# Key columns taken into the first modulation, a wide first MLP product, and a last panel that finishes token tile 0 first

## The chip, the cores and the metric

One core of one Trainium2 chip. The metric is the device time of one execution in microseconds (us); lower is better. Everything is float32 data; products run on TensorE (PE) in fp32r, each operand split into a high part (rounded to fp32r) and a low part (the rest), so that one product of the reference becomes three matmuls: high by high, high by low, low by high.

## What is computed

One layer of a trunk over 256 context and 256 latent tokens, width 2048 (biases, gates' details and norms left out):

```
mod_l, mod_c = silu(c) @ w_ada + b_ada, silu(c_ctx) @ w_ada + b_ada     # 6 x 2048 each
ul, uc  = (xl * (1 + sc1_l) + sh1_l) @ w_in, (xc * (1 + sc1_c) + sh1_c) @ w_in
ya, yb, yc = hgrn(uc, ul), pool(ul), attention(uc, ul)                  # attention: q, k, v are columns of w_in
xl = LayerNorm(ALPHA * xl + g1_l * (sum_j sigmoid(gate_j) * (y_j @ w_branch_j)) @ w_out)
h  = xl * (1 + sc2_l) + sh2_l
xl = LayerNorm(ALPHA * xl + g2_l * (square(relu(h @ w_ff1)) @ w_ff2))   # w_ff1 2048 x 8192
```

## The kernel before

All weights (395 MB) stream once from HBM in chunks of 1 MB: 512 rows by 512 columns, laid out 128 partitions x 4 row tiles x 512 columns. SyncE issues their DMAs in one fixed order (`stream()`), into a ring of eight slots during the first modulation and of four after it; each DMA waits until the chunk that held its slot is used up. Four chunks along the rows make a panel of 512 output columns.

A chunk of kind "s" is split in two halves: ScalarE (ACT) copies a half to `whi` (L405), VectorE (DVE) subtracts it from the raw half into `wlo` (L847), TensorE multiplies. `whi` and `wlo` hold four halves; a half's place is free when TensorE has ended the half four before it (counted by `w_used`, or by `blk_done` for a panel's last half). Chunks of kind "p" (`ada`) are the first two sixths of w_ada and are multiplied raw by a 32-column vector operand (L1356); ACT copies the sums out (`sums_out`, L426), TensorE turns them (`turn`, L1365), DVE makes the modulated inputs, whose high and low parts are `hCL`, context and latent side by side (512 columns). Chunks of kind "a" are the rest of w_ada and are summed on DVE (`ada_sum`, L865 and L868), beside later panels.

The first stage has four rounds `kc`, each with eight `ada` chunks. From the second on, a round also multiplies one chunk of the first value panel (`value_block`, L1375 to L1377), from inputs that the round before has modulated. ACT's order in a round is: sums out, split of the value chunk, sums out, high parts of `hCL`. After it come value chunk 3, the second value panel, then the panel of attention keys and values (L1285 to L1287 for the keys, L1453 to L1457 for the values), then 4 "forget" panels, queries, gates, branches, the output projection, and the MLP.

The MLP has four rounds `f`. In each, four panels of w_ff1 go through `features` (L1285 to L1287): the weights are the stationary operand, 128 columns at a time, the 256 latent tokens are the moving one. DVE takes each result through relu (L1189) into `sq`, GpSimd (POOL) squares it and makes its two parts `hid` (L831, L724, L726). Then four panels of w_ff2 go through `tokens` (L1324 to L1326): `hid` is stationary, 512 weight columns move, two token tiles `t` of 128 rows each. A tokens panel takes chunk n only when the `hid` rows of feature panel n are done, so the first of them needs the last feature panel's `hid` at its chunk 3. In the last panel of all, chunks 2 and 3 are done for tile 0 first and then for tile 1 (`apart=2`), so that DVE's closing work on tile 0 (`ff_out`, L1200 to L1207; `last_rows`, L1214 and L1216) runs beside tile 1.

Of the kernel before, what the change touches and what calls it, by code (L numbers as in the profile page):

```python
# [52 lines left out]
class Stream:  # L53
# [4 lines left out]
    def __init__(self):  # L58
        self.order, self.place, self.nth = [], {}, {}
        self.count = {"s": 0, "p": 0, "a": 0}  # L60
        self.split_order = []
# [3 lines left out]
    def add(self, kind, name, n, src, index):  # L65
# [9 lines left out]
        if kind == "s":  # L75
            self.split_order.append((name, n))

# [6 lines left out]
    def half(self, name, n, h):  # L84
        return 2 * self.nth[name, n] + h
# [6 lines left out]
def stream():  # L92
# [27 lines left out]
    for n, pan in enumerate((PAN_AI + 1, PAN_CKV)):  # L120
        for k in range(4):
            panel("vals", 4 + 4 * n, k, "w_in", 4 * pan + k)
            summed()
            summed()
    for n in range(16):
        panel("forget", n, 0, "w_in", 4 * PAN_AF + n)
        summed()
    for n in range(8):
# [28 lines left out]
class Panels:  # L157
# [8 lines left out]

    def add(self, name, first, chunks, banks, who):
# [15 lines left out]

def panels():
    pn = Panels()
    four = (0, 1, 2, 3)
    for first in (0, 4, 8):
        pn.add("vals", first, 4, four, "A")
# [13 lines left out]
    for f in range(4):  # L202
        for i in range(4):
            pn.add("mlp", 32 * f + 4 * i, 4, four, "V")
# [8 lines left out]
def build(nc, vecs, cst, rcnt, masks, xT, xtok, rows, w_ada, w_in, pool_w, w_br, w_out, w_f1, w_f2, outT):  # L213
    weights_of = {"w_ada": w_ada, "w_in": w_in, "w_br": w_br, "w_out": w_out, "w_f1": w_f1, "w_f2": w_f2}
    with ExitStack() as ctx:
# [11 lines left out]
        wlo = at("wlo", [P, 4, 2, PW], 48 * KB, F32R)  # L227

# [89 lines left out]
        def sem(name):  # L318
# [12 lines left out]
         m_tr, m_hi, m_lo, ax_in, var_in, rs_out, nm_out, h2_tr, h2_hi, h2_lo, x1_done, hid_lo, y_out, cleared) = (  # L331
# [5 lines left out]
            "m_tr m_hi m_lo ax_in var_in rs_out nm_out h2_tr h2_hi h2_lo x1_done hid_lo y_out cleared").split())  # L337
# [32 lines left out]
        def _(sp):  # L370
            for n, (kind, name, k, src, index) in enumerate(ST.order):
# [4 lines left out]
                if ST.holder[n] is not None:  # L376
# [3 lines left out]
                    elif was == "s":  # L380
                        sp.wait_ge(lo_made, ST.half(old, o, 1) + 1)
# [3 lines left out]
                sp.dma_start(slots[slot][:].rearrange("p a b -> p (a b)"),  # L385
# [7 lines left out]
        def _(act):  # L393
# [3 lines left out]
            def split(name, n, halves=(0, 1)):  # L397
                slot = ST.slot(name, n)
                act.wait_ge(raw_full[slot], ST.full(name, n))
                for h in halves:  # L400
# [4 lines left out]
                    nc.scalar.copy(whi[:, q % 4], slots[slot][:, 2 * h:2 * h + 2]).then_inc(hi_made, 1)  # L405
# [1336 lines left out]
```

## Time and profile before

| | |
|---|---|
| median of 3 runs | 1952.09 us (1946.99 to 1952.15) |
| the profiled execution | 1952.81 us, of which the traced span is 1951.0 us |
| TensorE busy | 1885.7 us (97%) |
| VectorE busy | 1258.3 us (64%) |
| ScalarE busy | 777.3 us (40%) |
| GpSimd busy | 389.3 us (20%) |
| HBM traffic | 409.04 MB, mean 210 GB/s |

TensorE's time runs through the whole span. In the timeline a matmul's length is its way through the array, longer than the distance between two starts; that distance is what one costs in a row of them, and is read from the starts.

### The profile page before, as it was taken

What the parts mean: (1) busy time and instruction counts of PE and PEld (TensorE: products, weight loads), DVE (VectorE), ACT (ScalarE), POOL (GpSimd) and SP (SyncE); (2) the same over time, 40 slices, a digit from 0 to 9 for tenths busy, and PEclk for the clock granted to TensorE, in tenths of its full rate; (3) what the DMA queues carried; (4) which work ended last, traced back from release to release, by engine and by line L of the source; (5) the groups of instructions that cost most, each with busy time, mean ns of one, the idle gap of its engine ahead of it and who ended that gap; (6) DMA issues with size and microseconds to landing.
All of it is one profiled execution on the core that took longest, in us unless ns stands there. A gap on an engine that the chain in (4) does not pass through costs nothing.

```text
span 1951.0 us, 26303 instructions
## 1 busy us (share of the span) xinstructions
PE 1885.7 (97%) x10808; PEld 1624.0 (83%) x10808; DVE 1258.3 (64%) x1438; ACT 777.3 (40%) x891; POOL 389.3 (20%) x325
## 2 busy tenths in 40 slices
PE   5999999999999999999999998999999999999996
PEld 1568887889999877887888887998998899889985
DVE  1247646786877776487676666766676467556686
ACT  1132224455555554444444435433333333333331
POOL 0000000002837343100010100450054024203500
PEclk7889999999999999999999999999999999999998
DMA  9957745555343454476676754666665566556652
GB/s 400 421 200 271 261 170 173 173 177 188 111 142 106 136 212 159 143 275 221 232 273 235 273 199 168 219 221 203 244 236 197 196 214 235 194 194 224 230 175 84
DMA packets 59319, 409.04 MB, mean 210 GB/s; under 512 B 6336, under 2 KB 9024, under 8 KB 10304
## 3 DMA queue, kind: packets, MB, share of 16 engines
q1 hardware_dynamic: 54720, 395.34, 57.2%
q10 hardware_dynamic: 4480, 12.02, 1.6%
q8 instruction: 86, 1.41, 0.3%
q14 instruction: 33, 0.27, 0.0%
HBM read 405.24 MB, written 2.10 MB: 209 GB/s over the span
## 4 chain that ended last, share of the span: by engine, by line
PE 86%; DVE 7%; DMA 2%; POOL 1%; DVEq 1%; issue 1%; ACT 1%; SPq 0%; ACTq 0%
PE main L1324 14%; PE main L1326 14%; PE main L1325 14%; PE main L1285 11%; PE main L1286 11%; PE main L1287 11%; DVE asum L868 2%; DMA raw<-in_w_ada 2%; PE main L1375 2%; DVE wlo L847 2%; PE main L1376 2%; PE main L1377 2%; PE side L1356 1%; PE side L1519 1%; PE side L1589 1%
## 5 line engine op out<-in xcount | busy, mean ns | idle before, releaser
L847 DVE TENSOR_TENSOR wlo<-raw,whi 128x1024 fp32r<-128x1024 f32 x552 | 722.3, 1334 | 329.8 <-ACT whi L405 329.2
L405 ACT CAST whi<-raw 128x1024 fp32r<-128x1024 f32 x552 | 574.1, 1050 | 792.8 <-PE main L1326 421.3
L1285 PE MATMUL main<-h,whi 128*128 128x256 f32 x1024 | 291.5, 285 | 4.6 <-DVE h L1180 2.5
L1286 PE MATMUL main<-h,whi 128*128 128x256 f32 x1024 | 291.1, 284 | 0.0
L1287 PE MATMUL main<-h,wlo 128*128 128x256 f32 x1024 | 291.0, 284 | 0.0
L1285 PE MATMUL main<-hCL,whi 128*128 128x256 f32 (+1 forms) x800 | 261.9, 327 | 7.1 <-DVE ya L1030 3.6
L1286 PE MATMUL main<-hCL,whi 128*128 128x256 f32 (+1 forms) x800 | 258.4, 323 | 0.0
L1287 PE MATMUL main<-hCL,wlo 128*128 128x256 f32 (+1 forms) x800 | 258.2, 323 | 0.0
L868 DVE SCALAR_TENSOR_TENSOR asum<-raw,sm,asum 128x512 f32<-128x512 f32 x240 | 192.6, 802 | 19.5 <-issue 0.4
L1324 PE MATMUL main<-whi,hid 128*128 128x512 f32 x512 | 201.2, 393 | 0.9 <-DVE wlo L847 0.9
L1285 PEld LDWEIGHTS main<-h,whi 128*128 128x128 f32 x1024 | 197.8, 193 | 5.1 <-DVE h L1180 2.8
L1325 PE MATMUL main<-wlo,hid 128*128 128x512 f32 x512 | 199.5, 390 | 0.0
L1326 PE MATMUL main<-whi,hid 128*128 128x512 f32 x512 | 199.5, 390 | 0.0
L1286 PEld LDWEIGHTS main<-h,whi 128*128 128x128 f32 x1024 | 197.7, 193 | 0.1
L1287 PEld LDWEIGHTS main<-h,wlo 128*128 128x128 f32 x1024 | 197.8, 193 | 0.0
L831 POOL TENSOR_TENSOR sq<-sq 128x256 f32<-128x256 f32 x64 | 67.5, 1055 | 535.6 <-DVE sq L1189 528.0
L1285 PEld LDWEIGHTS main<-hCL,whi 128*128 128x128 f32 x800 | 153.4, 192 | 18.9 <-issue 6.5
L1286 PEld LDWEIGHTS main<-hCL,whi 128*128 128x128 f32 x800 | 153.5, 192 | 11.2 <-issue 0.2
L1287 PEld LDWEIGHTS main<-hCL,wlo 128*128 128x128 f32 x800 | 153.3, 192 | 11.4
L1324 PE MATMUL main<-whi,hCL 128*128 128x512 f32 x384 | 156.2, 407 | 0.4 <-DVE wlo L847 0.4
L1326 PE MATMUL main<-whi,hCL 128*128 128x512 f32 x384 | 150.0, 391 | 0.0
L1325 PE MATMUL main<-wlo,hCL 128*128 128x512 f32 x384 | 149.8, 390 | 0.0
(226 smaller groups left out, 2631.2 us busy)
## 6 DMA issues: line engine op xcount, KB each, us to landing
raw<-in_w_f SPq DMA_DIRECT2D x128, 1024.0 KB, 4.9
raw<-in_w_in SPq DMA_DIRECT2D x108, 1024.0 KB, 4.9
raw<-in_w_ada SPq DMA_DIRECT2D x96, 1024.0 KB, 6.2
raw<-in_w_br SPq DMA_DIRECT2D x24, 1024.0 KB, 5.0
raw<-in_w_out SPq DMA_DIRECT2D x16, 1024.0 KB, 5.0
xin<-in_xT SPq DMA_DIRECT2D x4, 1024.0 KB, 18.2
ax<-in_xtok ACTq DMA_DIRECT2D x1, 2048.0 KB, 8.4
lng<-in_rows ACTq DMA_DIRECT2D x2, 1024.0 KB, 7.1
```

The lines of the kernel that those rows point to most:

```text
L405: nc.scalar.copy(whi[:, q % 4], slots[slot][:, 2 * h:2 * h + 2]).then_inc(hi_made, 1)
L831: TT(sq[:, b], sq[:, b], sq[:, b], ALU.mult)
L847: TT(wlo[:, q % 4], slots[slot][:, 2 * h:2 * h + 2], whi[:, q % 4].bitcast(F32), ALU.subtract).then_inc(lo_made, 1)
L868: last = STT(asum[:], slots[slot][:, j], s, asum[:], ALU.mult, ALU.add)
L1285: mm(out, w_hi, x_hi, start=start, stop=False)
L1286: mm(out, w_hi, x_lo, start=False, stop=False)
L1287: return mm(out, w_lo, x_hi, start=False, stop=stop)
L1324: mm(out, x[:, kt, 0, own], whi[:, par, j], start=start, stop=False)
L1325: mm(out, x[:, kt, 0, own], wlo[:, par, j], start=False, stop=False)
L1326: last = mm(out, x[:, kt, 1, own], whi[:, par, j], start=False, stop=stop)
L1375: mm(main[:, b], x[:, kt, 0, tile], whi[:, par, j], start=kt == 0, stop=False)
L1376: mm(main[:, b], x[:, kt, 0, tile], wlo[:, par, j], start=False, stop=False)
```

## The change

Three parts. **Keys:** the 512-column panel of attention keys and values is cut in two kinds of chunks: four `keys` chunks of half a megabyte (512 rows by 256 columns, one half each) and two `cv` chunks of 1 MB (1024 rows by 256 columns). Key chunks 0 to 2 are streamed, split and multiplied in the first stage, chunk 3 after value chunk 3; in PSUM they have banks 2 and 3 of `side`, and the modulation sums keep only bank 1, where they had 1 and 2. **Wide:** `features` in the MLP is replaced by `wide`; its results have the high-part and low-part sums in two halves of a bank, which ACT and DVE add, and the panels alternate between `main` and `side`. Squares are made by ACT (high part) and GpSimd. **Tail:** `apart=4` in the last panel, with places of their own for its last four halves (`whi_end`, `wlo_end`, where `h2` was).

```diff
@@ stream() @@
         if kc:
             panel("vals", 0, kc - 1, "w_in", 4 * PAN_AI + kc - 1)
+            st.add("s", "keys", kc - 1, "w_ck", kc - 1, halves=1)
...
+    st.add("s", "keys", 3, "w_ck", 3, halves=1)
@@ panels() @@
-            pn.add("mlp", 32 * f + 4 * i, 4, four, "V")
+            pn.add("mlp", 32 * f + 4 * i, 4, (four, SIDE)[i % 2], "V")
@@ scalar: split @@
-                    if q >= 4:
+                    if q == HALVES - 4:
+                        act.wait_ge(blk_done, PN.base["mlp", 108] + 4)
+                    elif 4 <= q < HALVES - 4:
                         which, count = PN.last[q - 4]
                         act.wait_ge(ended[which], count)
@@ scalar: first stage @@
-                nc.scalar.copy(am[:, n % 2], side[:, 1 + n % 2]).then_inc(am_out, 1)
+                nc.scalar.copy(am[:, n % 2], side[:, 1]).then_inc(am_out, 1)
...
                 split("vals", kc - 1)
+                split("keys", kc - 1)
@@ scalar: MLP @@
+            def hidden_in(f, i):
+                if f or i:
+                    act.wait_ge(hid_lo, 4 * f + i)
+                for b in range(4):
+                    blk("mlp", 32 * f + 4 * i, b)
+                    nc.scalar.copy(sq[:, b], (main, side)[i % 2][:, b, 0:T]).then_inc(hid_in, 1)
+
+            def hidden_high(f, i):
+                act.wait_ge(hid_pos, 4 * f + i + 1)
+                A(hid[:, 4 * i:4 * i + 4, 0], sq[:], ACT.Square).then_inc(hid_hi, 1)
...
                         split_after("mlp", 32 * f + n)
+                    if n in (4, 8, 12, 16):
+                        hidden_in(f, n // 4 - 1)
+                    if n in (5, 9, 13, 17):
+                        hidden_high(f, n // 4 - 1)
@@ gpsimd: MLP @@
+            for n in range(16):
+                pool.wait_ge(hid_hi, n + 1)
+                TT(sq[:], sq[:], sq[:], ALU.mult)
+                drain()
+                own = slice(n % 4 * 4, n % 4 * 4 + 4)
+                TT(hid[:, own, 1], sq[:], hid[:, own, 0].bitcast(F32), ALU.subtract).then_inc(hid_lo, 1)
@@ vector: hidden_out @@
-                    nc.vector.tensor_scalar_max(sq[:, b], main[:, b, 0:T], 0.0).then_inc(freed["V"], 1)
+                    dve.wait_ge(hid_in, 16 * f + 4 * i + b + 1)
+                    TT(sq[:, b], sq[:, b], (main, side)[i % 2][:, b, T:2 * T], ALU.add).then_inc(freed["V"], 1)
+                drain()
+                nc.vector.tensor_scalar_max(sq[:], sq[:], 0.0).then_inc(hid_pos, 1)
@@ tensor: new wide() @@
+                            for j in range(2):
+                                kt, own = 4 * n + 2 * h + j, slice(P * b, P * (b + 1))
+                                mm(ps[:, b], whi[:, par, j, own], h2[:, kt].rearrange("p v t -> p (v t)"),
+                                   start=kt == 0, stop=kt == 15, skip_group_check=True)
+                                last = mm(ps[:, b, 0:T], wlo[:, par, j, own], h2[:, kt, 0], start=False,
+                                          stop=kt == 15, skip_group_check=True)
@@ tensor: first stage @@
             for kc in range(1, 4):
                 for k in range(4):
                     ada_chunk(8 * kc + k)
+                    if kc > 1:
+                        key_block(kc - 2, k)
...
+            for k in range(4):
+                key_block(2, k)
@@ tensor: MLP @@
-                           between=lambda k: ada_spread(12 + f) if i == 0 and k == 0 else None,
-                           apart=2 if f == i == 3 else 0)
+                           between=lambda k: gate2(f) if i == 0 and k == 1 else None,
+                           apart=4 if f == i == 3 else 0)
```

Left out of the diff: the bookkeeping of halves, the new host layouts `w_ck` and `w_cv`, four of the `ada_sum` chunks that move from the panel of keys and values to the first forget panel (with two of their turns), DVE's matching splits, and the waits on the freed banks.

On TensorE, at the start of the third round of the first stage (`raw` is a slot, `side` bank 1 takes the modulation sums): four `ada` chunks before, then the value chunk.

```order
L1356 MATMUL side<-raw_50,sR 32x512 x4
L1356 MATMUL side<-raw_51,sR 32x512 x4
L1356 MATMUL side<-raw_52,sR 32x512 x4
L1356 MATMUL side<-raw_53,sR 32x512 x4
L1375 MATMUL main<-whi,hCL 128x512
```

The same place in the change, its first `ada` chunk and what follows.

```order
L1455 MATMUL side<-raw_51,sR 32x512 x4
L1360 MATMUL side<-hCL,whi 128x512
L1361 MATMUL side<-hCL,whi 128x512
L1362 MATMUL side<-hCL,wlo 128x512
L1360 MATMUL side<-hCL,whi 128x512
L1361 MATMUL side<-hCL,whi 128x512
L1362 MATMUL side<-hCL,wlo 128x512
L1455 MATMUL side<-raw_52,sR 32x512 x4
```

A quarter of a key chunk, six matmuls of 512 columns, stands behind each of the four `ada` chunks, the last of them ahead of the value chunk.

On TensorE, in the first feature panel of the MLP, before:

```order
L1285 MATMUL main<-h_79,whi 128x256
L1286 MATMUL main<-h_79,whi 128x256
L1287 MATMUL main<-h_79,wlo 128x256
L1285 MATMUL main<-h_79,whi 128x256
L1286 MATMUL main<-h_79,whi 128x256
L1287 MATMUL main<-h_79,wlo 128x256
```

And in the change:

```order
L1400 MATMUL main<-h_81,whi 128x512
L1402 MATMUL main<-h_81,wlo 128x256
L1400 MATMUL main<-h_81,whi 128x512
L1402 MATMUL main<-h_81,wlo 128x256
L1400 MATMUL main<-h_81,whi 128x512
```

Two matmuls stand where three stood, with the same 768 columns in all.

On GpSimd, the work for one feature panel before is four times these three rows:

```order
L831 TENSOR_TENSOR sq<-sq 128x256
L724 TENSOR_TENSOR hid<-sq,ones 128x256
L726 TENSOR_TENSOR hid<-sq,hid 128x256
L831 TENSOR_TENSOR sq<-sq 128x256
L724 TENSOR_TENSOR hid<-sq,ones 128x256
L726 TENSOR_TENSOR hid<-sq,hid 128x256
```

In the change it is these first two rows (and they repeat for each panel):

```order
L904 TENSOR_TENSOR sq<-sq 128x1024
L907 TENSOR_TENSOR hid<-sq,hid 128x4x256
L904 TENSOR_TENSOR sq<-sq 128x1024
L907 TENSOR_TENSOR hid<-sq,hid 128x4x256
L904 TENSOR_TENSOR sq<-sq 128x1024
```

Two operations of 1024 elements stand where twelve of 256 stood, and they start only when ACT's square of all four blocks is done.

## Rows read from the trace of the kernel before

**Rows 1.** The page: span, and TensorE's busy time (share, instructions)

```profile
span 1951.0 us, 26303 instructions
PE 1885.7 (97%) x10808; PEld 1624.0 (83%) x10808; DVE 1258.3 (64%) x1438; ACT 777.3 (40%) x891; POOL 389.3 (20%) x325
```

**Rows 2.** TensorE's waits, whole span: us in total, times, longest

```profile
PE main L1375 <- DVE wlo L847: 9.0, 3, 3.0
```

**Rows 3.** Stretches of the first stage: length, busy times, then PEclk, DMA share, GB/s

```profile
66.30:95.50 29.20, 26.20 (x130) 14.12 (x129) 8.06 (x17) 5.54 (x8) 0.00 (x0) 0.82 1.01 421
...
74.00:84.30 10.30, 10.30 (x36) 5.09 (x35) 0.00 (x0) 0.00 (x0) 0.00 (x0) 0.50 1.02 422
...
103.00:112.40 9.40, 9.40 (x35) 4.98 (x34) 2.40 (x3) 0.58 (x1) 0.00 (x0) 0.54 0.17 72
```

**Rows 4.** TensorE's timeline, first stage: start, length, what [idle before]

```profile
55.78 0.40 PE L1377 MATMUL main<-whi,hCL 128*128 128x512 f32 x1
56.11 1.07 PE L1356 MATMUL side<-raw,sR 128*32 128x512 f32 x8
57.11 0.50 PE L1375 MATMUL main<-whi,hCL 128*128 128x512 f32 x1
57.44 0.39 PE L1376 MATMUL main<-wlo,hCL 128*128 128x512 f32 x1
...
66.32 3.64 PE L1356 MATMUL side<-raw,sR 128*32 128x512 f32 x32
72.96 0.47 PE L1375 MATMUL main<-whi,hCL 128*128 128x512 f32 x1 [3.00 <-DVE wlo L847]
...
125.53 0.50 PE L1375 MATMUL main<-whi,hCL 128*128 128x512 f32 x1 [1.19 <-DVE hCL L902]
```

**Rows 5.** TensorE's timeline, MLP: 16 starts of 256 columns, 96 of 512

```profile
1212.03 0.28 PE L1287 MATMUL main<-h,wlo 128*128 128x256 f32 x1
...
1213.83 0.28 PE L1287 MATMUL main<-h,wlo 128*128 128x256 f32 x1
...
1912.37 0.39 PE L1324 MATMUL main<-whi,hid 128*128 128x512 f32 x1
...
1933.90 0.39 PE L1326 MATMUL main<-whi,hid 128*128 128x512 f32 x1
```

**Rows 6.** Two other idle times, and the granted clock around them

```profile
1229.40 0.36 PE L1285 MATMUL main<-h,whi 128*128 128x256 f32 x1 [2.05 <-DVE wlo L847]
...
1221.40:1235.00 13.60, 11.55 (x97) 11.38 (x96) 10.71 (x15) 7.76 (x11) 1.09 (x2) 1.00 0.66 233
...
319.50 1.70 PE L1469 MATMUL side<-cs,kctx 128*128 128x128 f32 x8 [2.57 <-ACT kctx L479]
...
320.00:330.00 10.00, 10.00 (x41) 0.84 0.32 105
```

**Rows 7.** Groups of DVE; then the squares' chain around 1304.34 (tokens start)

```profile
L1189 DVE TENSOR_SCALAR sq<-main 128x256 f32<-128x256 f32 x64 | 27.2, 425 | 35.3 <-PE main L1287 35.3
...
L868 DVE SCALAR_TENSOR_TENSOR asum<-raw,sm,asum 128x512 f32<-128x512 f32 x240 | 192.6, 802 | 19.5 <-issue 0.4
...
1310.01 1.05 ACT L405 CAST whi<-raw 128x1024 fp32r<-128x1024 f32 x1 [1.61 <-PE main L1326]
...
1302.96 0.61 POOL L831 TENSOR_TENSOR sq<-sq 128x256 f32<-128x256 f32 x1 [9.61 <-DVE sq L1189]
...
1305.37 1.40 POOL L831 TENSOR_TENSOR sq<-sq 128x256 f32<-128x256 f32 x1 [0.16 <-issue]
...
L779 POOL TENSOR_TENSOR qr<-qr,qs x2: 2377/2790/3204, 670.1 to 781.7; 128x1024 f32<-128x1024 f32 x2
```

**Rows 8.** DVE's timeline over the last panel and behind it

```profile
1915.51 4.81 DVE L847 TENSOR_TENSOR wlo<-raw,whi 128x1024 fp32r<-128x1024 f32 x4
...
1928.96 0.69 DVE L1200 TENSOR_TENSOR res<-main,g2b 128x512 f32<-128x512 f32 x1 [3.20 <-PE main L1326]
...
1938.68 0.68 DVE L1200 TENSOR_TENSOR res<-main,g2b 128x512 f32<-128x512 f32 x1
```

More of the change, by code:

```diff
@@ L76, in add @@
             self.split_order.append((name, n))
+            first = sum(count for _, count in self.halves.values())
+            self.halves[name, n] = (first, halves)
     def slot(self, name, n):
@@ L84, in half, with halves_of, split @@
     def half(self, name, n, h):
-        return 2 * self.nth[name, n] + h
+        return self.halves[name, n][0] + h
+    def halves_of(self, name, n):
+        return range(self.halves[name, n][1])
+    def split(self, name, n):
+        return sum(self.halves[name, n])
     def following(self, name, n):
@@ L165, in __init__, with together @@
         self.last, self.base, self.before, self.own = {}, {}, {}, {}
+    def together(self, banks, order, who):
+        for at, (name, n, h) in enumerate(order):
+            if all(later[0] != name for later in order[at + 1:]):
+                self.base[name, 0] = self.blocks
+                self.blocks += len(banks[name])
+                self.last[ST.half(name, n, h)] = ("blk_done", self.blocks)
+            else:
+                self.used += 1
+                self.last[ST.half(name, n, h)] = ("w_used", self.used)
+        for name, own in banks.items():
+            self.before[name, 0] = [None] * len(own)
+            self.own[name, 0] = self.emptied[who]
+            for b in own:
+                self.emptied[who] += 1
+                self.bank[b] = (who, self.emptied[who])
     def add(self, name, first, chunks, banks, who):
@@ L186, in panels @@
     four = (0, 1, 2, 3)
-    for first in (0, 4, 8):
-        pn.add("vals", first, 4, four, "A")
+    order = [half for n in range(4) for half in (("vals", n, 0), ("vals", n, 1), ("keys", n, 0))]
+    pn.together({"vals": four, "keys": ("side 2", "side 3")}, order, "A")
+    pn.add("vals", 4, 4, four, "A")
+    pn.add("cv", 0, 2, (2, 3), "A")
     for it in range(4):
@@ L380, in _ @@
                     elif was == "s":
-                        sp.wait_ge(lo_made, ST.half(old, o, 1) + 1)
+                        sp.wait_ge(lo_made, ST.split(old, o))
                     else:
@@ L917, in _ @@
                     split("vals", kc - 1)
+                    split("keys", kc - 1)
                 if kc == 3:
@@ L1386, in _, with key_block @@
             pe.wait_ge(silu_hi, 1)
-            for n in range(5):
+            def key_block(n, quarter):
+                b, pair = quarter // 2, quarter % 2
+                par = half_ready("keys", n, 0)
+                w_hi, w_lo = (w[:, par].rearrange("p a (c n) -> p (a c) n", c=2) for w in (whi, wlo))
+                for j in range(2):
+                    kt, own = 4 * n + 2 * pair + j, slice(P * b, P * (b + 1))
+                    last = three(side[:, 2 + b], w_hi[:, 2 * pair + j, own], w_lo[:, 2 * pair + j, own],
+                                 hCL[:, kt, 0], hCL[:, kt, 1], kt == 0, kt == KT - 1)
+                if n == 3 and pair == 1:
+                    last.then_inc(blk_done, 1)
+                elif quarter == 3:
+                    last.then_inc(w_used, 1)
+            for n in range(4):
                 ada_chunk(n)
             turn(0)
-            for n in range(5, 8):
+            for n in range(4, 8):
                 ada_chunk(n)
```

241 lines of the change are left out of this document (137 added, 104 removed).

## The prediction

> **What bounds the kernel now.** I read the page first: TensorE is busy for 97% of 1951.0 us [rows 1], so only three things can shorten the kernel: fewer or cheaper matmuls, less idle TensorE time before its end, or a shorter tail behind it. TensorE's waits come next. They are few: three of 3.00 us each for the low halves of the first value panel's chunks, and in the MLP one of 2.05 us [rows 2, 6]. The table of stretches then shows that the first stage loses more to the clock than to the waits: after the waits of 3.00 us the granted clock is 0.50 for 10.3 us and 0.54 for 9.4 us, the lower of its two levels (1.2 GHz, against 2.4) nearly throughout, while the work is the same [rows 3, 4]. DMA is also full there (share 1.01, 421 GB/s) [rows 3]. Last, starts in the timeline give what a matmul costs in a row of them: 15 steps of 256 columns in 1.80 us are 0.120 us each, 95 steps of 512 columns in 21.53 us are 0.2266 us [rows 5]. At 2.4 GHz the columns alone would take 0.1067 and 0.2133 us, so each matmul carries some 0.0133 us that do not depend on its columns.
>
> **Wide product.** 4 rounds x 4 panels x 16 row tiles x 4 blocks are 1024 triples. A triple costs 3 x 0.120 = 0.360 us; the pair should cost 0.2266 + 0.120 = 0.3466 us. That saves 0.0134 us, times 1024 = 13.7 us. The trace has no 256-column matmul behind a 512-column one of other weights. Bounds: nothing saved, if the pair takes 0.360; twice as much, 27 us, if the short one hides its fixed part and costs its columns alone. I take 13.7, since both measured lengths fit one fixed part.
>
> The Trainium skill (TensorE: Matmul & The Clock Gate, Back-to-back issue gap) gives a fixed part of only about 2.5 ns for an isolated warm matmul, and says that weight loads also set the spacing of real streams. By 2.5 ns the sum would be 2.6 us instead of 13.7. The 13 ns of this trace disagree with it, and I go by the trace.
>
> Two deductions in the first MLP round. The wait of 2.05 us is for DVE's modulated inputs and their splits, whose time does not move; three chunks (48 triples) stand ahead of it, so 0.6 us saved there only lengthens it, to 2.7. The clock stood at 1.00 around 2.05 us of idle time, but after 2.57 us it was 0.84 over 10 us, 1.6 us lost [rows 6]. I charge 1.6. The wide part is worth 13.7 - 0.6 - 1.6 = 11.5 us.
>
> What hides behind TensorE in a round: ACT's copies and square and DVE's four additions replace DVE's four relus (0.425 us each) [rows 7]; DVE is at 64% and ACT at 40% [rows 1]. In feature panels 1 to 3 a chain has a whole panel of 22 us. In the features part the panels alternate between two sets of banks, so none waits for a bank. The one tight place is the last feature panel, below.
>
> **Keys.** All 96 key matmuls of 512 columns stay; 72 of them (16.3 us) move from behind the stage into it. What changes for TensorE is only this:
> - In rounds 2 and 3, four `ada` chunks end and then 3.00 us pass until ACT has copied the sums and split, and DVE has made the low half [rows 4]. Now a key quarter stands behind the fourth chunk: 6 x 0.2266 + 0.1 = 1.5 us. The idle time falls to 1.5 us, 3.0 us in two rounds.
> - At 125.53 there was 1.19 us of idle time for the last modulated inputs; now key chunk 2 (5.4 us) stands in it. Gain 1.2 us.
> - Idle times of 1.19 and 2.05 us left the clock at 1.00, 2.57 us cost it a little, 3.00 us cost it all [rows 3, 4, 6]. At 1.5 us I expect no drop. The two low stretches lost 10.3 x 0.50 + 9.4 x 0.46 = 9.5 us [rows 3]; that comes back. The first low stretch, from round 1, has no keys ahead of it and stays.
> - Each switch between `ada` and ordinary matmuls costs: 0.33 us in place of 0.23 before, 1.00 in place of 0.91 (3.64 for four chunks) in it, 0.33 in place of 0.23 behind [rows 4]. That is 0.29 us, for eight new pairs 2.3 us.
>
> Sum: 3.0 + 1.2 + 9.5 - 2.3 = 11.4 us. Covers: a round's DMA becomes 10.5 chunks, 26.2 us at 421 GB/s, against TensorE's 29.2 us now and about the same later (29.2 - 1.5 - 5.2 + 5.4 + 1.2), so the key halves hide; without that cover three of them would cost 3.7 us. The single sums bank makes a sum's first chunk wait for ACT's copy; in rounds 1 to 3 a value block and the turn, which waits for that copy anyway, stand between, and round 0 waits for DMA. The four `ada_sum` chunks moved to the first forget panel find DVE idle: that panel has no gate work and lasts 192 x 0.2266 = 43.5 us, and eight sums (4 operations each, at most 0.80 us) [rows 7] and eight splits at 1.2 us [rows 8] take 35.
>
> **Tail.** The last panel starts at 1912.37; tile 0 ended after 72 matmuls, at 1928.7, and DVE began at 1928.96 and reached tile 1 only at 1938.68, though TensorE had ended at 1934.1 [rows 5, 8]. Now tile 0 takes 48 matmuls, 10.9 us, but its third half is needed at 1915.1 and DVE, busy with the panel before, makes it only from 1915.51 to 1916.7 [rows 8]: 1.6 us idle. The halves after it come every 1.2 us and are eaten every 1.36. Tile 0 ends at 1924.9, tile 1 at 1935.8. DVE's 9.7 us for tile 0 then run from 1925.2 to 1934.9, and tile 1 is taken when TensorE ends, at 1936.1 instead of 1938.7. Gain 2.5 us (tile 0's work is no longer the later one, the matmuls are). Bounds: 4.6 if the idle time does not come, a loss of about 2.5 if it drops the clock for 10 us.
>
> **Sum.** 11.5 + 11.4 + 2.5 = 25.4 us off the profiled execution's 1952.8: 1927.4. The median of the runs is 0.7 us below that execution, so 1927 is what I forecast.
>
> **The rivals.**
> - *The clock stays low in the first stage.* For it: each round begins with `ada` matmuls of 32 columns and 1.5 us of idle time remains. Against: the rows at 1.19 and 2.05 us. It costs 4.3 us for one stretch, 9.5 for both: 1931 to 1937. Chance 0.18.
> - *The pair costs what the triple did*, the short matmul being held by the weight load. For it: no row shows the pair; against: the fixed part is the same for both lengths. It gives 1927 + 11.5 = 1938.5. Chance 0.08. The skill's 2.5 ns would put it 2.6 us under that.
> - *The squares come late, clock kept.* Say a round's last feature panel ends at E. ACT's square is queued behind a split that waits for tokens chunk 0 and starts at E + 5.7 (1310.01) [rows 7]; with 1.05 for it and as much for the square, GpSimd starts at E + 7.8. Its two operations of 1024 elements take 2.4 to 3.2 us each, and each DVE split beside them adds 0.8 (1.40 against 0.61) [rows 7]; three or four of these give an end at E + 15.0 to 17.4. Chunk 3 of the first tokens panel is needed at E + 72 x 0.2266 = 16.3, somewhat later with the gate's matmul in between. I take no wait; the upper bound costs 1.1 us in four rounds, 4.4 us, and 2.5 us late would make 10: 1931 to 1937. Chance 0.09. The skill (GPSIMD Engine Reference, Specifications) says that GpSimd's SBUF interfaces contend with VectorE instructions of two SBUF inputs; the trace agrees, 1.40 us against 0.61.
> - *Slower: the squares come so late that the clock drops each time.* The same chain, ended at E + 19.3 or later, leaves TensorE idle for 3 us, which in the first stage cost 3.0 + 5.2 us. Four rounds cost 33 us, more than the 25 gained: 1960. It needs 1.9 us more than my upper bound. Chance 0.05.
> - *Keys are not absorbed*: the stage is DMA's after all, chunks come late and the 11.4 us do not appear: 1938. For it speaks the DMA share of 1.01, against it that TensorE's waits of 3.00 us are for DVE's work and not for DMA. Chance 0.04.
>
> **How the numbers follow.** The forecast has 0.56; its own range is 1921 to 1932 (the wide bound above, a switch cost or a small clock drop below). The range 1920 to 1938 takes in the first, third and last rival and leaves out about 0.13. 0.3% is 5.9 us, about what a measurement of this kernel can tell from no change: under 1946.2 counts as faster. Only the slower rival, and two of the others together, reach beyond it: faster 0.91, within 0.3% 0.04, slower 0.05.
>
> **What would show it.** Right: TensorE's waits at round starts of 1.5 us instead of 3.00 and a clock of 1.00 from about 55 us on; first value panel's chunk 3 starting near 130 us; pairs in the MLP starting 0.347 us apart and each MLP round 3.4 us shorter (the first 1.2); no wait of tokens for GpSimd's `hid`; tile 1's `ff_out` directly behind the last matmul. Wrong: a clock near 0.5 after 75 us, a pair of 0.36, tokens waiting for GpSimd at chunk 3, or DVE waits of TensorE in the forget panels.

## The result and the profile after

The changed kernel takes 1933.53 us (median of 6 runs, 1932.29 to 1933.79). The kernel before, run beside it, takes 1947.14 us (median of 6, 1943.45 to 1952.15). The ratio is 0.9925, with a 95% interval from 0.9909 to 0.9941: faster by 0.75%. It lies within the forecast range (1920 to 1938) and 6.5 us above the forecast of 1927.

Two differences must be kept apart. Between the medians lie 13.6 us, between the two profiled executions 19.3 us (1952.81 before, 1933.53 after): the profiled execution of before was one of its longest. Everything read from traces below adds up to the 19.3; the first experiment says where the other 5.7 come from.

The page of the changed kernel, beside [rows 1]: TensorE is as full as it was, with 1024 matmuls fewer.

```profile
span 1931.7 us, 23993 instructions
PE 1870.1 (97%) x9784; PEld 1562.1 (81%) x9784; DVE 1283.3 (66%) x1454; ACT 810.2 (42%) x971; POOL 277.5 (14%) x165
PEclk8999999999999999999999999999999999999999
L904 POOL TENSOR_TENSOR sq<-sq 128x1024 f32<-128x1024 f32 x16 | 31.6, 1975 | 659.3 <-ACT hid L761 659.3
```

**First stage.** The two stretches of [rows 3] and their successors in the changed kernel (length, busy time and count of PE, PEld, DVE, ACT and POOL, then granted clock, DMA share, GB/s):

```profile
44.20:54.50 10.30, 10.21 (x37) 6.03 (x37) 2.22 (x2) 0.58 (x1) 0.00 (x0) 0.54 1.01 421
66.30:95.50 29.20, 27.80 (x153) 15.94 (x152) 8.92 (x17) 6.37 (x9) 0.00 (x0) 1.00 1.02 421
95.50:124.40 28.90, 27.50 (x151) 15.54 (x150) 10.90 (x19) 8.01 (x11) 0.00 (x0) 1.00 0.87 352
```

From 66.30 to 95.50 the clock is 1.00 where it was 0.82, and TensorE runs 153 matmuls where it ran 130. In this stage only the stretch behind the first round's wait is still at 0.54, near the lower of the two levels. The waits of the second and third round are 1.40 us, close to the 1.5 that was counted on. Value chunk 3 starts at 130.67 where it started at 125.53 [rows 4], though 72 key matmuls (16.3 us) have been done before it: 11.2 us gained by then. (Timeline of TensorE; in brackets the idle time before; the rows from 1218.62 on are for the parts below.)

```profile
76.29 0.39 PE L1362 MATMUL side<-hCL,wlo 128*128 128x512 f32 x1
78.08 0.47 PE L1474 MATMUL main<-whi,hCL 128*128 128x512 f32 x1 [1.40 <-DVE wlo L919]
...
107.63 0.47 PE L1474 MATMUL main<-whi,hCL 128*128 128x512 f32 x1 [1.40 <-DVE wlo L919]
...
130.67 0.39 PE L1474 MATMUL main<-whi,hCL 128*128 128x512 f32 x1
...
1218.62 0.47 PE L1400 MATMUL main<-h,whi 128*128 128x512 f32 x1 [2.25 <-DVE wlo L919]
...
1418.65 0.40 PE L1400 MATMUL side<-h,whi 128*128 128x512 f32 x1
...
1422.18 0.40 PE L1400 MATMUL side<-h,whi 128*128 128x512 f32 x1
...
1899.92 0.47 PE L1423 MATMUL main<-whi,hid 128*128 128x512 f32 x1 [1.62 <-DVE wlo L919]
```

**The pair.** From 1418.65 to 1422.18 ten pairs start: 0.353 us each, not 0.3466. Over all starts from 1240 to 1900 the low matmul follows the wide one after 0.236 us (0.2266 in a row of wide ones) and the wide one follows the low one after 0.117 (0.120 in a row of low ones) [rows 5]: what is lost is lost on the wide matmul. The tokens panels of the four MLP rounds start at 1292.18, 1470.59, 1649.01 and 1827.42, so a round lasts 178.41 us; before they started at 1304.34, 1484.46, 1664.59 and 1844.72, 180.13 us apart. A round has 256 pairs: 0.360 - 1.715 / 256 = 0.3533 us for each.

That is not so everywhere. In two stretches of the first round, 1204.8 to 1209.7 and 1210.9 to 1215.8, the same alternation costs what its two parts cost; six pairs here take 2.08 us, 0.347 each:

```profile
1212.05 0.39 PE L1400 MATMUL main<-h,whi 128*128 128x512 f32 x1
...
1214.13 0.39 PE L1400 MATMUL main<-h,whi 128*128 128x512 f32 x1
```

`e7` has a longer such stretch.

**The square's chain**, at the first tokens panel (E = 1292.18), as the timelines of ACT, POOL and DVE show it:

```profile
1298.80 1.06 ACT L761 ACTIVATE hid<-sq 128x1024 fp32r<-128x1024 f32 x1
...
1299.93 1.98 POOL L904 TENSOR_TENSOR sq<-sq 128x1024 f32<-128x1024 f32 x1 [17.64 <-ACT hid L761]
1302.05 2.65 POOL L907 TENSOR_TENSOR hid<-sq,hid 128x1024 fp32r<-128x1024 f32 x1
...
1300.08 2.38 DVE L1299 TENSOR_TENSOR ax<-res,lng 128x512 f32<-128x512 f32 x1
1302.53 2.73 DVE L1301 TENSOR_TENSOR ax<-ax,lnb 128x512 f32<-128x512 f32 x1
```

GpSimd ends at 1304.7, that is E + 12.5, 3.8 us before chunk 3 needs `hid` at E + 16.3. In rounds 2 and 3 its second operation takes 3.19 us instead of 2.65 and it ends at E + 13.1. TensorE never waits for it.

**Tail**, DVE's timeline, beside [rows 8]:

```profile
1898.57 2.34 DVE L919 TENSOR_TENSOR wlo<-raw,whi 128x1024 fp32r<-128x1024 f32 x2
1900.83 4.62 DVE L919 TENSOR_TENSOR wlo_end<-raw,whi_end 128x1024 fp32r<-128x1024 f32 x4
1908.44 0.69 DVE L1275 TENSOR_TENSOR res<-main,g2b 128x512 f32<-128x512 f32 x1 [2.99 <-PE main L1425]
...
1919.25 0.69 DVE L1275 TENSOR_TENSOR res<-main,g2b 128x512 f32<-128x512 f32 x1 [1.01 <-PE main L1425]
```

The panel starts at 1895.42; tile 0 is taken 13.0 us later, tile 1 23.8 us later and after 1.01 us in which DVE was free and TensorE was not. Before, tile 1 was taken 26.3 us after the panel's start, with TensorE long done.

**Where the 19.3 us came from**, by three marks in both traces:

| part | before | after | gain | forecast |
| --- | --- | --- | --- | --- |
| start to the MLP's first feature matmul | 1206.09 | 1195.28 | 10.8 | 11.4 |
| from there to the start of the last panel | 706.3 | 700.1 | 6.1 | 11.5 |
| last panel's start to tile 1's `ff_out` | 26.31 | 23.83 | 2.5 | 2.5 |

### The profile page after: what moved, and what is told of

Its sections match the earlier page's. It is cut to its first block, busy times and chain, and to the rows that moved or that the text cites. A ratio compares the mean times of both kernels' runs of the same rounds, so it can differ in the third digit from the quotient of the medians.

```text
span 1931.7 us, 23993 instructions
## 1 busy us (share of the span) xinstructions
PE 1870.1 (97%) x9784; PEld 1562.1 (81%) x9784; DVE 1283.3 (66%) x1454; ACT 810.2 (42%) x971; POOL 277.5 (14%) x165
## 4 chain that ended last, share of the span: by engine, by line
PE 87%; DVE 7%; DMA 2%; issue 1%; POOL 1%; DVEq 1%; ACT 1%; SPq 0%; ACTq 0%
PE main L1423 14%; PE main L1424 14%; PE main L1425 14%; PE side L1400 6%; PE main L1400 6%; PE main L1360 4%; PE main L1362 4%; PE main L1361 4%; PE side L1402 3%; PE main L1402 3%; DVE asum L940 2%; DMA raw<-in_w_ada 2%; PE main L1474 2%; DVE wlo L919 2%; PE main L1476 2%; PE main L1475 2%
## 5 line engine op out<-in xcount | busy, mean ns | idle before, releaser
L919 DVE TENSOR_TENSOR wlo<-raw,whi 128x1024 fp32r<-128x1024 f32 x548 | 703.8, 1311 | 356.4 <-ACT whi L457 355.7
L1360 PE MATMUL main<-hCL,whi 128*128 128x256 f32 (+1 forms) x768 | 249.0, 324 | 8.0 <-ACT cq L623 4.4
L1362 PE MATMUL main<-hCL,wlo 128*128 128x256 f32 (+1 forms) x768 | 246.0, 320 | 0.0
L1361 PE MATMUL main<-hCL,whi 128*128 128x256 f32 (+1 forms) x768 | 245.8, 320 | 0.0
L940 DVE SCALAR_TENSOR_TENSOR asum<-raw,sm,asum 128x512 f32<-128x512 f32 x240 | 221.8, 924 | 19.5 <-issue 0.4
L1400 PE MATMUL main<-h,whi 128*128 128x512 f32 x512 | 183.8, 403 | 4.8 <-DVE h L1255 2.5
L1400 PE MATMUL side<-h,whi 128*128 128x512 f32 x512 | 181.3, 399 | 0.0
L1362 PEld LDWEIGHTS main<-hCL,wlo 128*128 128x128 f32 x768 | 147.5, 192 | 10.1
L1402 PE MATMUL main<-h,wlo 128*128 128x256 f32 x512 | 144.7, 283 | 0.0
L1402 PE MATMUL side<-h,wlo 128*128 128x256 f32 x512 | 143.8, 281 | 0.0
L904 POOL TENSOR_TENSOR sq<-sq 128x1024 f32<-128x1024 f32 x16 | 31.6, 1975 | 659.3 <-ACT hid L761 659.3
L1400 PEld LDWEIGHTS main<-h,whi 128*128 128x128 f32 x512 | 97.4, 190 | 29.4 <-DVE h L1255 2.8
L1400 PEld LDWEIGHTS side<-h,whi 128*128 128x128 f32 x512 | 96.2, 188 | 24.1
```

Source lines behind the costliest of these rows:

```text
L919: TT(half_at(q)[1], slots[slot][:, 2 * h:2 * h + 2], half_at(q)[0].bitcast(F32), ALU.subtract).then_inc(lo_made, 1)
L940: last = STT(asum[:], slots[slot][:, j], s, asum[:], ALU.mult, ALU.add)
L1360: mm(out, w_hi, x_hi, start=start, stop=False)
L1361: mm(out, w_hi, x_lo, start=False, stop=False)
L1362: return mm(out, w_lo, x_hi, start=False, stop=stop)
L1400: mm(ps[:, b], whi[:, par, j, own], h2[:, kt].rearrange("p v t -> p (v t)"), start=kt == 0, stop=kt == 15, skip_group_check=True)
```

## Experiments

The experiments were timed in three groups, each on another chip and beside the kernel before, whose medians there were 1947.34 us (`e1` to `e4`), 1945.06 (`e5` to `e8`) and 1946.51 (`e9` to `e11`). Kernels of different groups are therefore compared by their ratios, and sizes by the traces.

### e1: the kernel before, once more

No edit. Its runs spread over 9 us, those of the change over 1.5: is the clock of the first stage the reason?

> The kernel before, unchanged, profiled and timed once more. The first median of before was 1952.1 us, later runs of it lie at 1943 to 1947. Theory: its low-clock stretches in the first stage (0.50 for 10.3 us and 0.54 for 9.4 us) differ from execution to execution, since the work is the same; then this profile has fewer or shorter ones wherever its span is shorter, and the same start-to-start distances elsewhere. Rival: DMA or a later stage differs, and the first stage is the same 124 us to value chunk 3. A ratio of 1.000 within its interval.

Measured: 1944.81 us (median of 10 runs, 1943.1 to 1953.54), ratio 0.9994 [0.9977, 1.0011]. This profile was again of one of the longer executions (span 1951.8), with 0.82 from 66.30 to 95.50:

```profile
44.20:54.50 10.30, 9.54 (x32) 5.75 (x36) 1.75 (x2) 0.30 (x1) 0.00 (x0) 0.50 1.02 423
66.30:95.50 29.20, 26.20 (x129) 14.15 (x129) 8.09 (x18) 5.55 (x9) 0.00 (x0) 0.82 1.01 421
```

So the profile could not show a short one. The granted clock over the whole span, which every timed run records, does: runs at 0.981 have spans of 1950.9 to 1951.8 us, runs at 0.987 to 0.988 of 1941.3 to 1945.1. The kernel before comes up to 10 us shorter or longer with its clock. The profile from which I forecast was at the long end, and so a part of "the clock comes back" was already there in the runs that make the median. That agrees with the 5.7 us between 19.3 and 13.6; in which stretch the short runs keep their clock no trace shows.

### e2: the keys alone

The keys' part of the change; the MLP (`features`, not `wide`, with its squares on GpSimd) and the last panel as in the kernel before. In short:

```diff
-            pn.add("mlp", 32 * f + 4 * i, 4, (four, SIDE)[i % 2], "V")
+            pn.add("mlp", 32 * f + 4 * i, 4, four, "V")
...
-                           apart=4 if f == i == 3 else 0)
+                           apart=2 if f == i == 3 else 0)
```

> The keys part alone: first stage and panel of keys and values as in the change, MLP and last panel as before. From the two traces the keys part brought 10.8 us of the 19.3 us between the profiled executions. Theory (idle 3.00 to 1.40 us, clock kept): the MLP starts near 1195.3 us, as in the change, and the span is 1940 us; against the kernel before 5 to 11 us less, by how much of the low clock the runs of before show. Rival (the keys part only moves work and the gain was chance of the clock): same time as before within 3 us.

Measured: 1939.77 us (9 runs, 1939.33 to 1942.52), ratio 0.9964 [0.9951, 0.9977], span 1940.7. Tokens panels start at 1294.06 and 1474.19: rounds are 180.13 us as before, and the first of them is 10.3 us earlier than the kernel before had it. The clock from 66.3 to 124.4 is 1.00. Between profiles the keys are thus worth 10.3 us, between medians 7.6, and the spread falls from 12 us (the kernel before, beside it) to 3: most of what varied in the kernel before is gone with the keys' part.

### e5, e6: what a pair costs

Is the missing gain of the wide product a price of mixing two lengths, or does the new chain of ACT, DVE and GpSimd cost TensorE something? `e5` keeps the chain and cuts the wide matmul back in two; `e6` makes the low matmul 512 columns wide too, so that no lengths are mixed.

```diff
@@ e5_three_matmuls @@
-                                mm(ps[:, b], whi[:, par, j, own], h2[:, kt].rearrange("p v t -> p (v t)"),
-                                   start=kt == 0, stop=kt == 15, skip_group_check=True)
+                                for v in range(2):
+                                    mm(ps[:, b, T * v:T * (v + 1)], whi[:, par, j, own], h2[:, kt, v],
+                                       start=kt == 0 and v == 0, stop=kt == 15, skip_group_check=True)
@@ e6_low_wide @@
-                                last = mm(ps[:, b, 0:T], wlo[:, par, j, own], h2[:, kt, 0], start=False,
-                                          stop=kt == 15, skip_group_check=True)
+                                last = mm(ps[:, b], wlo[:, par, j, own], h2[:, kt].rearrange("p v t -> p (v t)"),
+                                          start=False, stop=kt == 15, skip_group_check=True)
```

> The change, with each 512-column matmul of the wide product cut back to two of 256 columns, so that the triple of before runs inside the new chain of banks, copies and squares. It separates the matmuls from the chain. Theory (the pair alone makes the gain): an MLP round from one start of tokens to the next is 180.1 us again, as before, instead of 178.4; span 6.7 us above the change's. Rival (the new chain costs TensorE something): the round is longer than 180.1 us.

> The change, with the matmul of the low weights 512 columns wide too (it adds low weights by low inputs, which neither kernel computes), so that all matmuls of the wide product have one length. Theory A (mixing lengths costs the 6.7 ns of a pair): the two cost 0.2266 us each, 0.4532 us a pair, and a round is 87.9 + 256 x 0.4532 = 203.9 us. Theory B (the wide matmul has a cost of its own, from its moving operand or from writing a whole bank): 0.233 us or more each, a round of 207.2 us or more.

Measured, `e5` (one run): 1942.04 us, span 1940.3. Tokens panels start at 1295.69, 1475.81, 1655.94 and 1836.07: rounds of 180.13 us, to the hundredth those of the kernel before. The new chain costs TensorE nothing; all that the wide product brings comes from the pair.

`e6` (one run): 2033.75 us, span 2032.0, rounds of 204.00 us. Against the 180.13 us of 256 triples that is 23.87 us more, so a pair takes 0.360 + 0.0932 = 0.4533 us, 0.2266 for each matmul. In TensorE's timeline:

```profile
1499.72 0.39 PE L1400 MATMUL side<-h,whi 128*128 128x512 f32 x1
1499.95 0.39 PE L1402 MATMUL side<-h,wlo 128*128 128x512 f32 x1
...
1501.08 0.39 PE L1400 MATMUL side<-h,whi 128*128 128x512 f32 x1
1501.31 0.39 PE L1402 MATMUL side<-h,wlo 128*128 128x512 f32 x1
```

Seven steps in 1.59 us, each as long as a step of 512 columns in [rows 5]. Two alternating lengths cost 6.7 ns a pair over the sum of their parts, two equal ones nothing. So the price comes with mixed lengths, and not with the other bank, the other weights or the longer chain. `e6` widens the low matmul's input and output along with its length, but in `e5` those change from one matmul to the next at one length, and nothing is lost there. Mixed lengths alone are not enough for it either: see the stretch above and `e7`.

### e3, e4, e10: fewer changes of length

If a change of length costs, grouping matmuls of one length should give it back. `e3` puts two wide and then two low ones, `e10` four and four, `e4` eight and eight; each sum gets the same products in another order.

```diff
@@ e3_pairs_grouped: for each block b @@
                             for j in range(2):
                                 mm(ps[:, b], whi[:, par, j, own], h2[:, kt].rearrange("p v t -> p (v t)"), ...)
+                            for j in range(2):
                                 last = mm(ps[:, b, 0:T], wlo[:, par, j, own], h2[:, kt, 0], ...)
@@ e4_eights_grouped: after the wide ones of all four blocks @@
+                        for b in range(4):
+                            for j in range(2):
                                 last = mm(ps[:, b, 0:T], wlo[:, par, j, own], h2[:, kt, 0], ...)
@@ e10_fours: the same with two blocks at a time @@
+                        for two in ((0, 1), (2, 3)):
```

> The change, with the order inside a block of the wide product altered: the two 512-column matmuls first, then the two 256-column ones, instead of 512, 256, 512, 256. The pair took 0.3533 us where 0.2266 + 0.120 = 0.3466 was forecast. Theory A: a change of length between neighbours costs the 0.0067 us; with half as many changes the four take 0.700 instead of 0.707 us and the kernel is 3.4 us faster than the change. Theory B: the 0.0067 us belong to the wide matmul itself (its moving operand, its output of a whole bank ahead of a second sum); nothing moves, 1931.7 us span.

> The change, with all eight 512-column matmuls of a half chunk (four blocks) ahead of its eight 256-column ones. Theory A: one eighth of the changes of length is left, 6.0 us faster than the change, span 1925.7 us. Theory B: nothing moves. A third reading, that the weights' reload and not the length counts, also moves nothing, since each matmul still has weights of its own.

> The change, with the matmuls of two blocks grouped: four of 512 columns, then four of 256. Rounds of the MLP were 178.42 us with the pairs alternating, 177.12 with groups of two and 177.34 with groups of eight; one fixed part per matmul would give 176.7. If groups of two are best because they end with the block's bank, groups of four lie at or above 177.1 to 177.3; if a longer group always loses less and the value of eight is an accident of its order, they lie at 176.9.

Measured: `e3` 1927.99 us (5 runs, 1927.16 to 1929.22), ratio 0.99 [0.9881, 0.9918]; `e4` 1928.2 us (6 runs, 1924.98 to 1929.88), ratio 0.9901 [0.9882, 0.9919]; `e10` in one run 1930.61. From the starts of the tokens panels in each trace, by 256 pairs to a round:

| order | round, us | pair, us | over 0.3466, ns |
| --- | --- | --- | --- |
| alternating (the change) | 178.42 | 0.3533 | 6.7 |
| twos (`e3`) | 177.12 | 0.3483 | 1.7 |
| fours (`e10`) | 177.78 | 0.3508 | 4.2 |
| eights (`e4`) | 177.34 | 0.3491 | 2.5 |

The timeline of `e3` shows two pairs from wide start to wide start in 0.70 us, 1418.75 to 1420.84 being three times that:

```profile
1418.75 0.63 PE L1401 MATMUL side<-h,whi 128*128 128x512 f32 x2
1419.22 0.39 PE L1405 MATMUL side<-h,wlo 128*128 128x256 f32 x2
1419.45 0.62 PE L1401 MATMUL side<-h,whi 128*128 128x512 f32 x2
...
1420.84 0.63 PE L1401 MATMUL side<-h,whi 128*128 128x512 f32 x2
```

and that of `e4` eight pairs from 1419.48 to 1422.27, 0.349 us each:

```profile
1419.48 2.00 PE L1400 MATMUL main<-h,whi 128*128 128x512 f32 x8
1421.32 1.12 PE L1405 MATMUL main<-h,wlo 128*128 128x256 f32 x8
1422.27 2.00 PE L1400 MATMUL main<-h,whi 128*128 128x512 f32 x8
```

Grouping in twos gives back three quarters of the loss: the ratio goes from 0.9925 to 0.99, some 5 us (the two intervals just overlap), and the traces say 4 x 1.30 = 5.2. But the loss does not fall with the number of changes of length. Twos have half of the changes and a quarter of the loss; fours have fewer changes than twos and a larger loss. So "a fixed price for each change" is refuted as the whole story; why twos are the best of the four no run here explains.

### e7: how long a wait the clock stands

The change puts a key quarter behind each `ada` chunk. `e7` puts it ahead, so that all the work is there but the wait ahead of the value chunk is 3.00 us again.

```diff
                 for k in range(4):
-                    ada_chunk(8 * kc + k)
                     if kc > 1:
                         key_block(kc - 2, k)
+                    ada_chunk(8 * kc + k)
```

> The change, with each key quarter ahead of its ada chunk instead of behind it, so that the fourth ada chunk again stands directly before the wait for the value chunk's split. The work is the same; the idle time should be 2.9 us again in rounds 2 and 3 instead of 1.40. Theory: the idle time sets the clock; 3 us more idle time, and the low clock comes back behind it in the profile (0.5 for about 10 us, twice), up to 9.5 us more, in the timed runs as often as in those of before: 3 to 12 us slower than the change. Rival: the clock stayed up because keys make the ada phase denser; then 3 us slower and the clock stays at 1.00.

Measured: 1939.16 us (12 runs, 1931.73 to 1941.85), ratio 0.9962 [0.9948, 0.9976]. TensorE's timeline and the stretches behind the two waits (columns as above):

```profile
78.76 0.47 PE L1474 MATMUL main<-whi,hCL 128*128 128x512 f32 x1 [3.00 <-DVE wlo L919]
...
112.82 0.47 PE L1474 MATMUL main<-whi,hCL 128*128 128x512 f32 x1 [3.00 <-DVE wlo L919]
```

```profile
80.00:95.50 15.50, 15.50 (x72) 8.82 (x72) 0.88 (x1) 0.59 (x1) 0.00 (x0) 0.80 1.01 420
95.50:110.00 14.50, 14.32 (x79) 8.14 (x77) 5.67 (x14) 2.60 (x5) 0.00 (x0) 1.00 0.86 332
110.00:124.40 14.40, 11.58 (x50) 6.59 (x50) 4.63 (x4) 4.25 (x5) 0.00 (x0) 0.76 0.81 317
```

The clock falls behind both waits and is back between them. The order of the key quarter is all that differs from the change: behind 1.40 us of idle time the clock stays at 1.00, behind 3.00 us it does not. With the idle time the order also changes what TensorE does just before it, an `ada` chunk here and a key quarter in the change; no run parts the two. The drop costs less here, 15.5 x 0.20 = 3.1 and 14.4 x 0.24 = 3.5 us, than it did before the change, 5.2 and 4.3 us [rows 3]. The ratio is 0.37% worse than the change's, 7 us. The spread of the runs is back too: 10 us, against 1.5 in the change and 13 in the kernel before beside it. In `e1` the clock over the whole span went with the length; here it does not, for two runs at 0.988 have spans of 1929.9 and 1939.9 us. Why `e7` spreads is open.

Between the profiles `e7` is only 4.2 us longer (1935.9 against 1931.7), though idle time and clock make 3.2 + 6.6 = 9.8. At the wait for `kctx` (308.06 in the change, 316.37 here) 8.3 us of them are there. Some 2.4 go by the MLP's start: the change's profile has two low stretches in the branches that this one lacks (below, in the part on why). And 1.4 go in the first MLP round, where all pairs behind its wait cost what the forecast had. The 208 pairs from 1224.13 to the tokens panel at 1296.32 take 72.19 us, 0.347 each; in the change they take 73.56. Ten of them:

```profile
1250.22 0.39 PE L1400 MATMUL side<-h,whi 128*128 128x512 f32 x1
...
1253.68 0.39 PE L1400 MATMUL main<-h,whi 128*128 128x512 f32 x1
```

From the second round on the pairs of this run take 0.3533 again. The order of the matmuls in the MLP is that of the change throughout. So the same alternation runs at 0.347 or at 0.353 us a pair, with nothing in the program between the two; what decides it no run here shows.

### e9: the last panel as it was

The change, with the last panel completing tile 0 over its last two chunks only.

```diff
-                           apart=4 if f == i == 3 else 0)
+                           apart=2 if f == i == 3 else 0)
```

> The change with apart=2 in the last panel again (chunks 0 and 1 for both tiles, then chunks 2 and 3 for tile 0 and for tile 1); the places of their own for the last halves stay. It undoes the tail part. Theory: tile 1 is taken 26.3 us after the panel's first matmul, as before, instead of 23.8, TensorE has no wait of 1.62 us, and the kernel is 2.5 us slower than the change. Rival (the tail part only trades DVE's lateness against TensorE's): the same time within 1 us.

Measured: 1933.56 us (6 runs, 1930.33 to 1936.05), ratio 0.9936 [0.9921, 0.995]. By ratios the tail is worth 1.1 per mille, 2 us, and the intervals overlap: alone, the timed runs do not tell it from nothing. The trace does. TensorE has no wait of 1.62 us, and DVE's timeline has the order of before again, with tile 1 right behind tile 0's work:

```profile
1910.15 0.69 DVE L1275 TENSOR_TENSOR res<-main,g2b 128x512 f32<-128x512 f32 x1 [6.56 <-PE main L1425]
...
1919.19 0.75 DVE L1291 SCALAR_TENSOR_TENSOR res<-res,rs,lnb 128x512 f32<-128x512 f32 x1
1919.86 0.68 DVE L1275 TENSOR_TENSOR res<-main,g2b 128x512 f32<-128x512 f32 x1
```

The panel starts at 1893.56, so tile 1 is taken after 26.3 us, as before, and 2.5 us later than in the change.

### e11, e8: what was left on the table

Two waits of the change are for DVE's low halves at places where the split stands behind something less urgent. `e11` lets ACT split ahead of its copy of the sums. `e8` adds the pairs in twos and lets DVE make the last splits ahead of the additions for the panel before.

```diff
@@ e11_early_split and e8_three_edits @@
-                sums_out(2 * kc)
                 split("vals", kc - 1)
+                sums_out(2 * kc)
@@ e8_three_edits, DVE @@
-                        if 32 * f + n < 127:
+                        if 32 * f + n < 123:
...
+            for t in range(2):
+                ff_out(3, 2, t)
             for t in range(2):
                 ff_out(3, 3, t)
```

> The change with only ACT's split of a round's value chunk ahead of its copy of the sums. In the version with three edits the waits of 1.40 us at the starts of rounds 2 and 3 were gone and the 2.98 us of round 1 stayed. Theory: 2.8 us less than the change, 1930.7 us. Rival: the three edits owed this step nothing and the other two gave more than their 5.1 and 1.8 us; then 1933.5 us.

> A version that the results point to: the change with grouped pairs (5.1 us by the rounds' lengths), ACT's split of the value chunk ahead of its copy of the sums (idle 3.00, 1.40 and 1.40 us at the starts of rounds 1 to 3 gone, and with the first of them perhaps the low clock from 44 to 54 us, up to 5 us), and DVE's closing work of the last but one panel behind all splits of the last (idle 1.62 us gone, tile 1 taken 1.8 us sooner). Theory: 1933.5 - 5.1 - 5.8 - 1.8 = 1921 us, with the clock 1916. Rival: the split ahead of the copy moves the sums and the turns back and nothing is gained there: 1926 us.

Measured: `e11` 1928.57 us (6 runs, 1927.73 to 1929.54), ratio 0.9912 [0.9898, 0.9926], span 1925.9. `e8` 1921.27 us (4 runs, 1920.78 to 1922.45), ratio 0.9878 [0.986, 0.9895], span 1920.7. In both, the waits of 1.40 us are gone. TensorE's timeline in `e11`:

```profile
44.16 0.77 PE L1474 MATMUL main<-whi,hCL 128*128 128x512 f32 x1 [2.99 <-DVE wlo L919]
...
76.89 0.50 PE L1474 MATMUL main<-whi,hCL 128*128 128x512 f32 x1
```

Its stretches (columns as above):

```profile
44.20:54.50 10.30, 10.30 (x51) 6.06 (x52) 2.17 (x2) 0.93 (x1) 0.00 (x0) 0.85 1.02 423
66.30:95.50 29.20, 29.20 (x163) 16.65 (x156) 9.98 (x19) 7.91 (x11) 0.00 (x0) 1.00 1.02 421
```

And TensorE's waits for `wlo` in `e8` (in total, times, longest):

```profile
PE main L1479 <- DVE wlo L919: 3.0, 1, 3.0
PE main L1362 <- DVE wlo L919: 2.5, 2, 1.2
PE main L1403 <- DVE wlo L919: 2.2, 1, 2.2
PE main L1428 <- DVE wlo L919: 1.2, 2, 0.8
```

The two waits at L1362 stand in the branches, at 518 and 617 us, and are not of these edits: the change has 2.26 and 2.19 us there, and `e9`, which is the same up to there, 2.19 and 1.25. The split ahead of the copy is worth 1.3 per mille, 2.5 us by ratios, near the 2.8 us of the two waits; the two intervals overlap, so that the waits are gone is shown by the trace, and their worth in time less surely. The wait of the first round, which I had expected to go too, stays at 2.99: there it is not ACT's copy that delays the split, and what does is not shown. The granted clock behind that wait was 0.60 in `e8`'s profile and 0.85 in `e11`'s, and up to there the two kernels are the same, so single profiles differ there by 10.3 x 0.25 = 2.6 us with no difference in the kernel. `e8` is the best version: 0.9878 against the change's 0.9925, some 9 us; the two waits, 5.2 us from the pairs and the 1.62 us in the last panel make 9.6.

## Why the prediction was near, and where it missed

**The keys were right, in mechanism and size.** Forecast 11.4 us, measured 10.8 between profiles, and 10.3 alone (`e2`). The idle time became 1.40 us instead of the 1.5 worked out; the clock stayed at 1.00 from about 55 us to the end of the stage. `e7` shows that the added matmuls alone do not keep it there; the shorter idle time, with the key quarter right before it, does. Value chunk 3 started at 130.67, near the 130 of the forecast. The halves hid behind TensorE: the waits at the value chunks are for DVE, as before. What I had not seen is that the low clock was not the same in every run. Measured against the median of the runs of before, not against one profile, the part was worth 7.6 us.

**The wide product: the mis-sized term.** "The pair should cost 0.2266 + 0.120 = 0.3466 us", since "both measured lengths fit one fixed part", was the step that failed. The pair takes 0.3533 nearly everywhere. The 1024 pairs save 1024 x 0.0067 = 6.9 us, not 13.7. The fixed part does hold for equal lengths (`e6`: 0.2266 each, with alternating weights); for alternating lengths it holds only in some stretches, two short ones in the change and nearly the whole first round in `e7`. So 0.3466 was a value that the pair can have, and the error was to count on it for all 1024 with no row of a mixture. I had both bounds (0.360 and the short one's columns alone) and took the value that needed no new cost. The Trainium skill (TensorE: Matmul & The Clock Gate, Back-to-back issue gap) has a fixed part of 2.5 ns for an isolated warm matmul; as an estimate from that page, the saving would have been 2.6 us. The measured 6.9 lies between that and mine, but for another reason, since rows of equal length keep their 13 ns [rows 5].

**Its deductions.** The wait in the first MLP round grew to 2.25 us, not 2.7: half the saving, half the lengthening. The 1.6 us charged for the clock did not come: over the 10 us behind that wait it is 1.00. In part that is luck. The same profile has 0.83 over the 10 us behind each of two waits of the same length in the branches, 2.26 us at 519.89 and 2.19 at 619.61, and behind 2.83 us at 1191.64 and 2.53 at 1195.28, which the kernel before has too, it has 0.74 (columns as above):

```profile
519.89:529.89 10.00, 10.00 (x72) 10.00 (x73) 9.91 (x8) 6.47 (x8) 8.23 (x5) 0.83 0.40 135
1195.28:1205.28 10.00, 10.00 (x46) 8.73 (x47) 6.10 (x9) 5.35 (x10) 0.00 (x0) 0.74 0.49 175
1218.62:1228.62 10.00, 10.00 (x57) 8.69 (x58) 7.39 (x10) 4.24 (x7) 0.00 (x0) 1.00 0.87 324
```

So 6.9 - 0.2 = 6.7 us were to be had, and 6.1 are seen. The starts of the tokens panels give 1.35 + 3 x 1.71 = 6.5; the last 0.35 us is a wait for DVE's low half in the last round, 0.79 us at 1878.98 where the kernel before has 0.44.

**The new chain cost TensorE nothing**, as the cover said: `e5` has the rounds of before to 0.01 us. Both rivals with late squares fall, and by more room than I gave them: GpSimd ended at E + 12.5 to 13.1, not at 15.0 to 17.4, with 1.98 and 2.65 to 3.19 us for its two operations. The contention that I charged to GpSimd showed on DVE instead.

**The tail was right in each number**: 1.62 us of idle time (1.6), tile 0 at 13.0 us (12.8), tile 1 2.5 us earlier (2.5), no clock drop. `e9` takes it away and the 2.5 us are back.

Together: 10.8 + 6.1 + 2.5 = 19.4 us for 25.4. The term of the pair alone was 6.8 us short; the sum missed by only 6.0 because the 1.6 us charged for the clock, which did not come, covered part of it. That the profile of before stood 5.7 us over the median of its runs beside the change did not shift the forecast: the change's runs stand at its own profile, 1933.5.

## What to carry to other kernels

Two matmul lengths measured each in its own row do not price a mixture: measure the mixture, over whole rounds and not over a few pairs, before counting on a fixed part per matmul, and try the same matmuls in groups. An idle time of 3 us on TensorE cost more here than itself, and not the same in each run; work that shortened it to 1.4 us bought the time, the clock and a smaller spread. Before a forecast is set against one profile, look at the spread of the runs and at where in it that profile stands.

## What the runs showed of the hardware

- Alternating 512 and 256 columns costs 6.7 ns a pair over the sum of the two; in twos 1.7, in fours 4.2, in eights 2.5. Two matmuls of 512 with alternating weights cost nothing beyond theirs. In some stretches (1204.8 to 1215.8 in the change, 1224 to 1296 in `e7`) the same alternation costs nothing beyond the sum. The pattern is open.
- Behind idle times of 1.40 and 1.62 us the granted clock stayed at 1.00. Between 2.05 and 2.6 us it went either way: 1.00 over 10 us behind 2.25 us at 1218.62 and 2.60 at 308.06, 0.83 behind 2.26 at 519.89 and 2.19 at 619.61, all in one profile of the change. Behind the first round's 3.00 us it was 0.50 to 0.85 for the next 10 us in the profiles taken, and 0.60 and 0.85 in two kernels that are the same up to there.
- An addition of 512 elements on DVE took 2.38 and 2.73 us beside GpSimd's long operations (0.68 and 0.69 for the same two lines at 1393.12 in the trace of before, where GpSimd is idle). The Trainium skill (GPSIMD Engine Reference, Specifications) says that the two contend; here DVE was the one that paid, by a factor of up to four, and TensorE did not wait for it.
